# Expert and memory weight slabs of whole rows, four a partition, with strips by column parity and the gated product transposed

## The reference, cut to what matters

```python
def expert_choice_ffn(h, w_router, w_gate_e, w_up_e, w_down_e):   # E = 16, D = FF = 1024
    cap = CAPACITY_FACTOR * N // N_EXPERTS                          # 32 tokens an expert
    aff = jax.nn.softmax((h @ w_router).astype(jnp.float32), axis=-1)
    top_aff, top_idx = lax.top_k(aff.transpose(0, 2, 1), cap)
    xg = h[bidx, top_idx]
    a = jnp.einsum("becd,edf->becf", xg, w_gate_e)
    u = jnp.einsum("becd,edf->becf", xg, w_up_e)
    out = jnp.einsum("becf,efd->becd", jax.nn.silu(a) * u, w_down_e) * top_aff[..., None]
    return jnp.zeros_like(h).at[bidx, top_idx].add(out)

def memory_cross_attention(hn, mem_n, w_xq, w_xkv, w_xo):
    k, v = jnp.split(mem_n @ w_xkv, 2, axis=-1)                     # w_xkv: 1024 x 1024
    ...
```

## Time and profile before

| what | before |
| --- | --- |
| median of 3 runs | 2202.5 us (2201.71, 2202.5, 2204.44) |
| the profiled execution | 2207.12 us, its span 2205.1 us |
| TensorE, matmuls (PE) | 1942.6 us busy, 88% of the span |
| TensorE, weight loads (PEld), beside the matmuls | 1078.1 us, 49% |
| VectorE (DVE) | 783.0 us, 36% |
| ScalarE (ACT) | 434.0 us, 20% |
| GpSimd (POOL) | 28.4 us, 1% |
| bytes moved by DMA | 575.39 MB in 133,730 packets, mean 261 GB/s |
| TensorE's granted clock, mean | 0.962 of full speed |
| instruction records | 29,899 |
| chain that ended last | PE 71%, DMA 22%, the rest 7%; of the DMA, 17% of the span is waits for `w_up_e` |

### The profile page before, as it was taken

The page is one execution under the profiler, slowest core; times in us unless marked ns, Lnnn a source line. Parts: engine busy times, 40 slices in busy tenths (PEclk is TensorE's granted clock), DMA queues, the critical chain, the costliest instruction groups (busy, mean ns, idle before and its releaser), DMA issues.

```text
span 2205.1 us, 29899 instructions
## 1 busy us (share of the span) xinstructions
PE 1942.6 (88%) x12755; PEld 1078.1 (49%) x12755; DVE 783.0 (36%) x1744; ACT 434.0 (20%) x1107; POOL 28.4 (1%) x54
## 2 busy tenths in 40 slices
PE   7999999999988989889999975667767699999998
PEld 4444544456433344335768641234324147764766
DVE  2587765344212122223354320211001135533543
ACT  2122711013111111003251110100000023221322
POOL 3000000000000000000000000000000000000000
PEclk9999999999999999999999987889989899999999
DMA  9644225415999999994317579999999943334230
GB/s 293 226 174 146 106 104 206 187 38 215 404 423 423 424 422 421 423 415 153 141 59 286 222 307 424 424 416 418 416 415 417 417 161 112 115 115 152 77 124 20
DMA packets 133730, 575.39 MB, mean 261 GB/s; under 512 B 7480, under 2 KB 16160, under 8 KB 92640
## 3 DMA queue, kind: packets, MB, share of 16 engines
q1 hardware_dynamic: 129312, 556.82, 63.6%
q0 software_dynamic: 3776, 16.48, 2.2%
q10 hardware_dynamic: 512, 0.19, 0.0%
HBM read 572.41 MB, written 1.05 MB: 260 GB/s over the span
## 4 chain that ended last, share of the span: by engine, by line
PE 71%; DMA 22%; DVE 3%; issue 2%; ACT 1%; SPq 0%; DVEq 0%; ACTq 0%
DMA ring<-w_up_e 17%; PE ps L865 10%; PE ps L1249 7%; PE ps L1307 6%; PE ps L1215 6%; PE ps L854 5%; PE ps L1029 4%; PE ps L881 4%; PE ps L1315 3%; PE ps L1474 3%; PE ps L1080 2%; DMA ring<-w_xkv 2%; DMA ring<-w_down_e 2%; PE ps L1181 2%; PE ps L1400 1%
## 5 line engine op out<-in xcount | busy, mean ns | idle before, releaser
L1215 PE MATMUL ps<-ring,reg_bc 128*32 128x512 f32 x2896 | 375.4, 659 | 148.4 <-DMA ring<-w_up_e 148.4
L1215 PEld LDWEIGHTS ps<-ring,reg_bc 128*32 128x32 f32 x2896 | 89.0, 116 | 410.8 <-DMA ring<-w_up_e 238.5
L865 PE MATMUL ps<-reg_a,ring 128*128 128x512 f32 (+1 forms) x768 | 253.7, 487 | 0.0
L2445 DVE TENSOR_TENSOR xall<-xall,ps 128x512 f32<-128x512 f32 x48 | 32.8, 687 | 451.3 <-PE ps L1181 451.3
L865 PEld LDWEIGHTS ps<-reg_a,ring 128*128 128x128 f32 x768 | 143.8, 190 | 96.3 <-issue 86.7
L2488 DVE TENSOR_TENSOR reg_a<-ps,reg_e 32x256 f32<-32x256 f32 x192 | 80.7, 420 | 192.0 <-PE ps L1249 189.5
L1307 PE MATMUL ps<-ring,reg_a 128*128 128x512 f32 (+2 forms) x448 | 141.7, 472 | 0.9 <-ACT reg_bc L1856 0.7
L1819 ACT ACTIVATE reg_bc<-ps 128x512 f32<-128x512 f32 x47 | 28.1, 597 | 571.2 <-PE ps L1215 571.2
L1249 PE MATMUL ps<-ring,reg_bc 128*32 128x256 f32 x2048 | 116.9, 380 | 14.3 <-issue 13.3
L854 PE MATMUL ps<-ring,reg_a 128*128 128x512 f32 (+1 forms) x288 | 112.5, 545 | 0.4 <-DVE reg_a L2063 0.4
L1307 PEld LDWEIGHTS ps<-ring,reg_a 128*128 128x128 f32 x448 | 75.2, 191 | 60.2 <-issue 58.5
(11 more groups left out here) (386 smaller groups left out, 2321.1 us busy)
## 6 DMA issues: line engine op xcount, KB each, us to landing
ring<-w_down_e SPq DMA_DIRECT2D x64, 2048.0 KB, 15.6
ring<-w_gate_e SPq DMA_DIRECT2D x123, 1024.0 KB, 11.2
ring<-w_up_e SPq DMA_DIRECT2D x123, 1024.0 KB, 14.3
ring<-w_in SPq DMA_DIRECT2D x34, 2048.0 KB, 9.2
ring<-w_ada SPq DMA_DIRECT2D x24, 2048.0 KB, 11.1
ring<-w_out SPq DMA_DIRECT2D x8, 2048.0 KB, 8.2
ring<-w_xkv SPq DMA_DIRECT2D x8, 1024.0 KB, 15.9
ring<-w_br_global SPq DMA_DIRECT2D x4, 1024.0 KB, 7.8
```

The lines of the kernel that those rows point to most:

```text
L865: mm = pe.matmul(ps[j][:, 0:n], w[:, k, j * P:(j + 1) * P], HT[:, k, 0:n], start=(k == 0), stop=(k == KC - 1))
L1215: mm = pe.matmul(ps[s][32 * j:32 * j + 32, :], XGT[l][:, e // 4, s, 2 * q + k, e % 4 * CAP:(e % 4 + 1) * CAP], w[j // 2][:, k, (j % 2) * C ...
```

## The change

**Gate and up apart, whole rows.** Slab 0 and 1 are the two halves (512 rows) of the gate matrix, slab 2 and 3 those of the up matrix; each has four whole rows a partition, 16 KB, and one DMA. `paired(k)` becomes `fours(k)`: every fourth column of 512, for gathers, transposes, modulation vectors, router and memory norm.

**Strips by half and parity.** `gate_up()` does 16 matmuls of 256 columns for a slab and set; strip j takes the columns of half j // 2 with parity j % 2, so the moving operand is read with a step of two. Gate sums go to columns 0 to 255 of the bank, up sums to 256 to 511.

**The product is turned, not its factors.** ScalarE takes the sigmoid straight from PSUM, VectorE multiplies by gate and by up into `ROW` (128 x 256); two transposes (`turn_row`) instead of four; ScalarE copies them to `HE`. The copy of 512 columns to `GU` falls away. The second set's transposes in layer 0 stand inside the first down slab; layer 0's scatter stands behind the first set's.

**Memory slabs.** Four of 2 MB (512 whole rows, 16 KB a partition) at experts 6, 8, 10 and 12. Each has all 1024 columns but half of the rows, so both slabs of a layer add into the same four banks: 16 matmuls of 256 columns for keys and 8 of 512 for values a slab, with two clearing matmuls of 512 columns ahead of a layer's first. The first slab's slot is freed at the end of its work (`mem_used`), the second's at the last `mem_side`; ScalarE copies four banks out after the second.

**Smaller things.** The second gathered half is waited for at slab 1 rather than slab 2. In layer 1 gathers, weight transposes and scatters use bank 6 alone (bank 7 is the memory's), except the first gather and the last scatter. The three modulation vectors and the memory norm's gain come in fours by two more small loads and two more copies at the start.

The diff, cut to its core:

```diff
-MEMORY_FROM = 6
+MEMORY_AT = (6, 8, 10, 12)
...
-            if l and 0 <= e - MEMORY_FROM < 8:
-                plan.append(("xkv", (e - MEMORY_FROM) // 4, (e - MEMORY_FROM) % 4))
+            if l and e in MEMORY_AT:
+                plan.append(("xkv",) + divmod(MEMORY_AT.index(e), 2))
...
-    def paired(k):
-
-        return slice(k // 2 * 2 * P + k % 2, (k // 2 + 1) * 2 * P, 2)
+    def fours(k):
+
+        return slice(k // 4 * 4 * P + k % 4, (k // 4 + 1) * 4 * P, 4)
...
-                return [(c0, 2, D, a[name][l, e, 2 * P * part:2 * P * (part + 1), :].rearrange("(p k) n -> p k n", p=P))
-                        for c0, name in ((0, "w_gate_e"), (2 * D, "w_up_e"))]
+                name, h = ("w_gate_e", "w_up_e")[part // 2], part % 2
+                return [(0, 4, D, a[name][l, e, 4 * P * h:4 * P * (h + 1), :].rearrange("(p k) n -> p k n", p=P))]
...
-            return [(0, KC, SEQ, kcol(a["w_xkv_2"][l], s * SEQ, SEQ))]
+            return [(0, 4, D, a["w_xkv_2"][l, 4 * P * s:4 * P * (s + 1), :].rearrange("(p k) n -> p k n", p=P))]
...
-            return at("mem_side", 8 * l + 2 * s + 2)
+            return at("mem_side", 4 * l + 4) if s else at("mem_used", l + 1)
...
+    def gather_bank(l, g, h):
+
+        return 6 if l and g else 6 + h
+
+    def scatter_bank(l, turn, n):
+
+        return 6 if l and turn < 3 else 6 + n % 2
...
+            def gate_up(bank, q, kept, w):
+
+                for k in range(4):
+                    for j in range(4):
+                        c = j // 2 * COL + j % 2
+                        mm = pe.matmul(ps[bank][32 * j:32 * j + 32, q // 2 * SEQ:(q // 2 + 1) * SEQ],
+                                       kept[:, 4 * (q % 2) + k, :], w[k // 2][:, k % 2, c:j // 2 * COL + COL:2],
+                                       start=(q % 2 == 0 and k == 0), stop=(q % 2 == 1 and k == 3))
+                return mm
+
+            def turn_row(e, s):
+
+                pe.wait_ge(*at(f"row@{l}", e * ns + s + 1))
+                if e:
+                    pe.wait_ge(*at(f"hid@{l}", (e - 1) * ns + s + 1))
+                for c in range(2):
+                    mm = pe.transpose(ps[2 + s][:, c * P:(c + 1) * P], ROW[l][:, s, c:SEQ:2], ident[:, :])
+                mm.then_inc(sem(f"row_turned@{l}"), 1)
+
+            def halves(i):
+
+                return [slot(i)[:, 2 * D * n:2 * D * (n + 1)].rearrange("p (k n) -> p k n", k=2) for n in range(2)]
...
-                    if q % 2 == 0 and e % 4 == 0:
-                        pe.wait_ge(*at(f"xgt@{l}", (e // 4 + 1) * 2 * ns - 1 + q // 2))
+                        w = halves(i)
+                    if q < 2 and e % 4 == 0:
+                        pe.wait_ge(*at(f"xgt@{l}", (e // 4 + 1) * 2 * ns - 1 + q))
                     for s in range(ns if l or e else 1):
                         if q == 0 and e:
-                            pe.wait_ge(*at(f"gu_read@{l}", ns if e == 1 else (e - 1) * ns + s + 1))
-                        for k in range(2):
-                            for j in range(4):
-                                mm = pe.matmul(ps[s][32 * j:32 * j + 32, :],
-                                               XGT[l][:, e // 4, s, 2 * q + k, e % 4 * CAP:(e % 4 + 1) * CAP],
-                                               w[j // 2][:, k, (j % 2) * COL:(j % 2 + 1) * COL],
-                                               start=(q == 0 and k == 0), stop=(q == 3 and k == 1))
+                            pe.wait_ge(*at(f"row@{l}", (e - 1) * ns + s + 1))
+                        mm = gate_up(s, q, XGT[l][:, e // 4, s, :, e % 4 * CAP:(e % 4 + 1) * CAP], w)
                         if q == 3:
...
-                if l and 0 <= e - MEMORY_FROM < 8:
-                    memory_groups((e - MEMORY_FROM) // 4, (e - MEMORY_FROM) % 4)
-                if e >= 4:
+                if l and e in MEMORY_AT:
+                    memory_groups(*divmod(MEMORY_AT.index(e), 2))
+                if l and e >= 4:
                     scatter(e // 4 - 1, range(e % 4 * ns, (e % 4 + 1) * ns))
-                for s in range(ns):
-                    pe.wait_ge(*at(f"gu_read@{l}", e * ns + s + 1 if e else ns))
-                    if e:
-                        pe.wait_ge(*at(f"hid@{l}", (e - 1) * ns + s + 1))
-                    for c in range(4):
-                        mm = pe.transpose(ps[2 + s][:, c * P:(c + 1) * P], GU[l][:, s, c:COL:4], ident[:, :])
-                    mm.then_inc(sem(f"gu_turned@{l}"), 1)
+                turn_row(e, 0)
+                if l == 0 and e >= 4:
+                    scatter(e // 4 - 1, range(e % 4 * ns, (e % 4 + 1) * ns))
                 for q in range(2):
                     i = where[("expert", l, 6 * e + 4 + q)]
                     slab_wait(pe, i)
                     w = slab_view(i, 4, D)
                     for s in range(ns):
                         if q == 0:
+                            if s:
+                                turn_row(e, s)
                             pe.wait_ge(*at(f"hid@{l}", e * ns + s + 1))
...
-            w = slab_view(i, KC, SEQ)
+            w = slab_view(i, 4, D)
             slab_wait(pe, i)
             pe.wait_ge(*at("mem_turned_read", 4))
-            for c in range(2):
-                n = 8 * layer + 2 * part + c
-                if n >= 3:
-                    pe.wait_ge(*at("mem_side_read", n - 2))
-                for k in range(KC):
-                    if part >= 2:
-                        mm = pe.matmul(ps[(1, 3, 5)[n % 3]][:, 0:SEQ], MEMT[layer][:, k, c * P:(c + 1) * P], w[:, k, :],
-                                       start=(k == 0), stop=(k == KC - 1))
-                    else:
-                        mm = pe.matmul(ps[(1, 3, 5)[n % 3]][:, 0:SEQ], w[:, k, c * P:(c + 1) * P], MEMT[layer][:, k, :],
-                                       start=(k == 0), stop=(k == KC - 1))
-                mm.then_inc(sem("mem_side"), 1)
+            if layer and part == 0:
+                pe.wait_ge(*at("mem_side_read", 4))
+            if part == 0:
+                for b in (1, 3):
+                    pe.matmul(ps[b][:, :], ident[:, :], pick[:, 1:2].broadcast_to([P, 512]), start=True, stop=False)
+            for c in range(4):
+                for k in range(4):
+                    mm = pe.matmul(ps[1 + c // 2 * 2][:, c % 2 * SEQ:(c % 2 + 1) * SEQ], w[:, k, c * P:(c + 1) * P],
+                                   MEMT[layer][:, 4 * part + k, :], start=False,
+                                   stop=(part == 1 and k == 3 and c % 2 == 1))
+                if part and c % 2:
+                    mm.then_inc(sem("mem_side"), 1)
+            for t in range(2):
+                for k in range(4):
+                    mm = pe.matmul(ps[5 + 2 * t][:, :], MEMT[layer][:, 4 * part + k, t * P:(t + 1) * P], w[:, k, COL:D],
+                                   start=(part == 0 and k == 0), stop=(part == 1 and k == 3))
+                if part:
+                    mm.then_inc(sem("mem_side"), 1)
+            if part == 0:
+                mm.then_inc(sem("mem_used"), 1)
...
+            def sigmoid(e, s):
+                m = e * ns + s
+                act.wait_ge(*at(f"up_done@{l}", m + 1 if e or l else 2 - s))
+                if e:
+                    act.wait_ge(*at(f"rg@{l}", m - ns + 1))
+                act.activation(EG[l][:, s, :], ps[5 if (l, e, s) == (0, 0, 1) else s][:, 0:SEQ], ACT.Sigmoid
+                               ).then_inc(sem(f"eg@{l}"), 1)
...
+                    act.wait_ge(*at(f"row_turned@{l}", m + 1))
+                    if e:
+                        act.wait_ge(*at(f"down@{l}", m - ns + 1))
+                    act.activation(HE[l][:, s].rearrange("p c m -> p (c m)"), ps[2 + s][:, 0:SEQ], ACT.Copy
+                                   ).then_inc(sem(f"hid@{l}"), 1)
...
-                    turned = ps[2 + s][:, :].rearrange("p (c n) -> p c n", c=4)
-                    dve.wait_ge(*at(f"eg@{l}", m + 1))
-                    dve.tensor_tensor(RG[l][:, s], EG[l][:, s], turned[:, :, 0:2 * CAP], ALU.mult
-                                      ).then_inc(sem(f"rg@{l}"), 1)
+                    got = ps[5 if (l, m) == (0, 1) else s]
+                    dve.wait_ge(*at(f"eg@{l}", m + 1 if e or l else 2 - s))
+                    dve.tensor_tensor(RG[l][:, s, :], EG[l][:, s, :], got[:, 0:SEQ], ALU.mult).then_inc(sem(f"rg@{l}"), 1)
                     dve.wait_ge(*at(f"rg@{l}", m + 1))
                     if e:
-                        dve.wait_ge(*at(f"down@{l}", m - ns + 1))
-                    dve.tensor_tensor(HE[l][:, s], RG[l][:, s], turned[:, :, 2 * CAP:4 * CAP], ALU.mult
-                                      ).then_inc(sem(f"hid@{l}"), 1)
+                        dve.wait_ge(*at(f"row_turned@{l}", m - ns + 1))
+                    dve.tensor_tensor(ROW[l][:, s, :], RG[l][:, s, :], got[:, SEQ:2 * SEQ], ALU.mult
+                                      ).then_inc(sem(f"row@{l}"), 1)
```

(50 more changed lines are left out.)

70 lines of the change are left out of this document (33 added, 37 removed).

## The result

The changed kernel takes 2238.43 us (median of 5, 2234.54 to 2240.29), the kernel before 2201.71 in the same runs: a ratio of 1.0160, interval 1.0148 to 1.0173, or 36.7 us more. The profiled execution took 2240.29 us, 33.2 more than that of before. The sign was right; 13.5 us had been forecast, and the time is 7 us above the range.

What follows compares the result with a forecast made beforehand. Expert stages were taken as bound by bytes through the DMA ring. Terms -8.6 - 3.6 + 20 + 4.4 + 0.5 + 0.8 = +13.5 us gave 2216 us for the median, range 2202 to 2231.

Steps and rivals of the forecast that it cites:

- Products by parity: Gate/up products at a step of two: 7.7 us a set for 7.07, hidden by weight waits; gathers in fours free.
- Memory slabs, order: Layer 1's memory experts: longer TensorE pieces free slots late, so the queue runs empty: +20 us, bounds 0 and 30.
- Rival 1: Memory slab's slot in layer 1: queue hides the pieces, the +20 falls away, -6.4 us, 2196; chance 0.14.
- Memory slabs, bytes: Layer 1's memory transfers: four 2 MB slabs in 16 KB rows replace eight of 1 MB, -3.6 us.
- Slabs of 16 KB rows: Gate and up slabs in both expert stages land 4.90 us apart for 4.97: -8.6 us, bounds 0 and -11.
- The rest: Small terms: TensorE's order after layer 0's last slab +0.5 us, some 5,800 more instruction records by bytes +0.8.
- The cover: Layer 0's experts: weight waits of 2.9 us an expert hide the longer products, with 1.0 left.
- Rival 2: Layer 0's products: the step of two costs more and TensorE becomes the bound, 22 us on top, 2238; chance 0.10.
- Start of layer 0: Before the queue is in step TensorE is the bound, so longer products show: +4.4 us, bounds 1.5 and 7.

Runs made afterwards that it cites:

- the two runs on it: Changed kernel with gathers and their transposes reading adjacent columns: 2221.58 us; kernel before with gathers alone reading every fourth column: 2214.22 us.
- the late release: Changed kernel with adjacent gathers and eight 1 MB memory slabs, each memory slab's slot held until the next expert's first gate slab was used: 2261.23 us.
- the version with both edits: Changed kernel with gathers reading adjacent columns and eight memory slabs of 1 MB at experts 6 to 13: 2199.65 us, ratio 0.9987.
- Split: Kernel before with nearly every gate/up product of 512 columns done as two of 256, slabs unchanged: 2205.86 us, ratio 1.0012.
- the idle instructions: Kernel before with 9,000 long-fulfilled waits added on GpSimd in the two expert stages: 2211.63 us, ratio 1.0054.

## Why the prediction was wrong, and where right

**The step that failed** is the last of "Products by parity": "So rows in fours in gathers and transposes cost nothing over pairs." It read three lines of transposes, where a load takes 209 ns at a step of two and of four, and carried that to the gathers, which are no transposes. Their own loads, 196 ns at two, became 330 at four. The term was 0; it is 11.7 us at layer 0's start and 2.7 at layer 1's (7.55 us for 4.87), and the two runs on it moved the time by 16.9 and 12.8. Without that step the changed kernel takes 2221.6 us, inside the range. The nearest row for a gather was the gather's own, with its step, and with no row at four the bound should have been open upward. The prediction named the rule that spoke against it and set it aside: the Trainium skill ("SBUF — State Buffer", the cacheline note in its section on the DMA port swizzle) wants two hits in a 16-byte line, which a step of four floats does not give; the gathers agree with it (192, 196, 330 ns at steps of one, two and four), while the transposes' loads (140, 209, 209) do not follow it. Why the two kinds differ was not tried.

**Memory slabs, order** was right as a mechanism and small in size: 30.1 us where 20 was taken, at the upper bound of 30. The main reason is the one that the bound named. The pieces are 17.3, 15.3, 17.3 and 15.4 us for 15.8 and 14.1, because they begin at the low clock (granted 0.61 in the first clearing matmuls, which take 3.18 us where 1.7 was forecast). The late slabs behind the first cost 2.0 to 2.9 a piece rather than 1.1: behind the first and third piece the down product runs partly at the low clock as well (5.35 and 5.33 us for 3.66), behind the second a gather at the step of four (4.00 us) stands between the two down slabs; behind the fourth the down product is at full speed (3.66), and why its slab needed 10.3 us is open. Issue at the end of the piece and a share of 0.61 are as forecast; the landing, 8.0 to 8.4 us behind the issue, is close to the 8.6. Rival 1 (the queue hides the pieces) is refuted by the changed kernel's windows and by the late release.

**Memory slabs, bytes:** -3.6 forecast; in the version with both edits the eight slabs take 19.7 us for 23.4, -3.7.

**Slabs of 16 KB rows** was right slab by slab and wrong in the sum. The median gap between gate and up landings falls from 4.97 to 4.90 in layer 0, as forecast, but the mean only from 5.05 to 5.04: the late landings grew. In the version with both edits the spacing gives 4.2 us over both stages (by the table, 1.7 in layer 0 and 6.2 in layer 1, less 3.7 of the memory's bytes), where -8.6 + 0.8 stood for slabs and records together. The step in doubt is "The rest", which priced records by their bytes; the page counts 125 blocks for 102:

```profile
q8 instruction: 125, 2.05, 0.4%
```

That these blocks are the cause is not shown: Split, with 122 of them, is inconclusive, and the idle instructions went through another queue. What the DMA records of the last thirteen experts of layer 0 show is where the late landings lie. In the changed kernel five slabs land 1.3 to 1.4 us late, 75 us apart, 6.8 us in all; in the kernel before eleven land 0.3 to 0.6 late, 5.4 in all. Each time a block was fetched between 1 us before the landing of the slab ahead and the late landing itself; but most blocks pass without a late slab, so there is no fixed price for a block.

**Products by parity:** a set takes 7.49 us, 7.7 forecast, 7.07 before. Most of the rise is the step of two: in Split, where nearly all columns come in adjacent 256s, a set of expert 0 takes 7.11. The cover held: in layer 0 the products still wait for weights, 1.35 us an expert against 2.9 in the earlier trace rows, and 1.0 was forecast. Rival 2 is refuted. By lines, 620 to 980, twelve experts:

```profile
L1123 PE MATMUL ps<-ring,reg_bc 128*32 128x256 f32 x3133 | 184.1, 389 | 16.2 <-DMA ring<-w_up_e 10.3 <-DMA ring<-w_gate_e 5.9
```

**Start of layer 0:** +4.4 forecast. Without the gathers' step it is -1.5 in the trace, but 2.5 us of that comparison is luck of the clock: the first gather of the kernel before ran partly at the low one, 6.59 us for 4.04. Without that luck it would be about +1 for the longer products and all else, not 4.4.

With the measured terms the sum is -4.2 - 3.7 + 30.1 - 1.5 + 11.7 + 2.7 = +35.1, beside 33.2 in the profiled executions. The terms come from several single executions, in which the clock fell at different places, so an agreement within 2 us is partly luck.

## What to carry to other kernels

Before a step of an access pattern is called free, look at the operand that it falls on and at the kind of instruction: a row of another kind, even on the same engine with the same step, is no price. In a ring of slots the latest moment to give a slot back is the time that the slabs ahead still fill, less the part of a fresh transfer's latency that is not transfer; a piece of work that keeps a slot should be cut until it ends before that. Adding instructions in a stage that lives on bandwidth may not be free either, as the idle ones here were not: look at their fetches.

## What the runs showed of the hardware that was not expected

- The stationary loads of a float32 128x128 matmul take 192 ns adjacent, 196 at a step of two floats and 330 at four; those of a transpose 140, 209 and 209. At the low clock (granted 0.50) the first take about 330 ns at a step of two and of four alike.
- 36 more fetches of 8 KB of instructions by an idle engine's queue cost 10.2 us in stages that are full of transfers, where their bytes would take 0.7.
- A 2 MB slab issued into an empty queue was in use 8.0 to 8.6 us later in the cases read here, of which 4.9 is its transfer.
